# Other order of weight loads and modulation products in a hybrid recurrent/PEER layer, one core

## What is computed

```python
mod = silu(c) @ w_mod + b_mod                       # 6 x 1024 values for each of two condition vectors
sh1, sc1, g1, sh2, sc2, g2 = split(mod, 6)
h = rmsnorm(x, norm1_g) * (1 + sc1) + sh1
xr, yr, xp, ga, gb = split(h @ w_in)                # 1024, 1024, 512, 1024, 1024 columns
xr = dwconv(xr)
hf, hb = rglru(xr, forward), rglru(xr, backward)    # gates by block-diagonal products, then a scan
branch_a = ((hf + hb) * gelu(yr)) @ w_up_rnn
branch_b = pool_mix(xp) @ w_up_pool
m = (sigmoid(ga) * branch_a + sigmoid(gb) * branch_b) @ w_o
x = x + g1 * m
h = rmsnorm(x, norm2_g) * (1 + sc2) + sh2
x = x + g2 * peer(h, wq, keys, u_tab, v_tab)        # product-key top-k, experts
y = rmsnorm(x, final_g)
```

## Time and profile before

| what | us |
|---|---|
| median of three runs | 2393.9 (2392.54 to 2401.06) |
| the profiled execution | 2405.23 |
| its span, first to last instruction | 2403.4 |
| TensorE busy in the span | 2281.8 |
| VectorE busy | 1691.7 |
| ScalarE busy | 817.3 |
| GpSimd busy | 980.9 |

### The profile page before, as it was taken

The page is one execution under the profiler, slowest core; times in us unless marked ns, Lnnn a source line. Parts: engine busy times, 40 slices in busy tenths (PEclk is TensorE's granted clock), DMA queues, the critical chain, the costliest instruction groups (busy, mean ns, idle before and its releaser), DMA issues.

```text
span 2403.4 us, 36139 instructions
## 1 busy us (share of the span) xinstructions
PE 2281.8 (95%) x11708; PEld 1947.9 (81%) x11708; DVE 1691.7 (70%) x3334; ACT 817.3 (34%) x1034; POOL 980.9 (41%) x578
## 2 busy tenths in 40 slices
PE   6799997999999999998999999998999999999995
PEld 2789987999999888786888888886888888888883
DVE  2549996131499999101888998997777777777775
ACT  1445553111323222222544444442222222222221
POOL 0223322222132444443222222225667666676671
PEclk9899998989799999999999999998999999999997
DMA  6412223333422444444688888877888888888881
GB/s 247 177 49 66 62 62 112 117 112 117 123 62 79 138 143 140 137 142 146 218 300 302 308 311 301 313 245 234 271 268 268 271 270 268 268 273 268 267 252 70
DMA packets 232787, 467.29 MB, mean 194 GB/s; under 512 B 115344, under 2 KB 115728, under 8 KB 231056
## 3 DMA queue, kind: packets, MB, share of 16 engines
q1 hardware_dynamic: 176416, 270.82, 36.6%
q0 software_dynamic: 36864, 134.23, 16.1%
q10 hardware_dynamic: 19440, 61.35, 6.4%
HBM read 402.37 MB, written 63.97 MB: 194 GB/s over the span
## 4 chain that ended last, share of the span: by engine, by line
PE 74%; issue 9%; DVE 6%; DMA 5%; POOL 3%; ACT 2%; DVEq 1%; ACTq 0%; SPq 0%; POOLq 0%
PE P L653 30%; PE P L457 19%; PE P L619 15%; POOL wLo L399 3%; PE P L642 3%; DMA rows<-in_u_tab,Eg 3%; PE P L479 3%; PE P L466 1%; PE P L543 1%; DMA gel_scratch<-gel 1%; DMA raw<-in_wblk 1%; PE P L499 1%; DVE ohA L1323 1%; DVE gq L1118 1%; DVE rows L1304 1%
## 5 line engine op out<-in xcount | busy, mean ns | idle before, releaser
L678 ACT ACTIVATE wHi<-raw 128x1024 fp32r<-128x1024 f32 x330 | 346.2, 1049 | 1354.2 <-PE P L653 509.6
L399 POOL TENSOR_TENSOR wLo<-raw,wHi 128x1024 fp32r<-128x1024 f32 x192 | 466.5, 2430 | 417.1 <-ACT wHi L678 416.9
L1366 DVE TENSOR_TENSOR wfLo<-wf,wfHi 128x512 fp32r<-128x512 f32 x128 | 313.8, 2452 | 165.4 <-ACT wfHi L678 165.4
L653 PE MATMUL P<-wfHi,wHi 128*128 128x512 f32 x1024 | 409.7, 400 | 10.2 <-DVE wfLo L1366 10.2
L619 PE MATMUL P<-hHi,wHi 128*128 128x512 f32 x1024 | 411.2, 402 | 3.7 <-DVE wLo L1311 3.2
L619 PE MATMUL P<-hHi,wLo 128*128 128x512 f32 x1024 | 406.3, 397 | 0.0
L653 PE MATMUL P<-wfHi,wLo 128*128 128x512 f32 x1024 | 404.4, 395 | 0.0
L619 PE MATMUL P<-hLo,wHi 128*128 128x512 f32 x1024 | 403.7, 394 | 0.0
L653 PE MATMUL P<-wfLo,wHi 128*128 128x512 f32 x1024 | 402.4, 393 | 0.0
L393 POOL TENSOR_TENSOR wLo<-raw,wHi 128x1024 fp32r<-128x1024 f32 (+1 forms) x76 | 182.6, 2404 | 502.4 <-ACT wHi L678 502.3
L418 POOL DMA_INDIRECT rows<-in_u_tab,Eg x128 | 134.6, 1052 | 357.4 <-DVE rows L1304 336.0
(11 more groups left out here) (172 smaller groups left out, 3264.2 us busy)
## 6 DMA issues: line engine op xcount, KB each, us to landing
raw<-in_ublk SPq DMA_DIRECT2D x128, 512.0 KB, 3.7
raw<-in_v_tab SPq DMA_DIRECT2D x128, 512.0 KB, 3.8
raw<-in_wblk SPq DMA_DIRECT2D x116, 512.0 KB, 3.7
gel_scratch<-gel ACTq DMA_DIRECT2D x128, 256.0 KB, 2.0
gsr<-gel_scratch SPq DMA_DIRECT2D x128, 256.0 KB, 6.2
gate_scratch<-stage ACTq DMA_DIRECT2D x6, 4096.0 KB, 17.0
gsr<-gate_scratch SPq DMA_DIRECT2D x128, 192.0 KB, 5.2
x<-in_xT SPq DMA_DIRECT2D x1, 2560.0 KB, 12.3
```

What stands on the lines that cost most here:

```text
L399: pool.tensor_tensor(wLo[:, j % 2, :], raw[:, j, :], wHi[:, j % 2, :].bitcast(f32), ALU.subtract).then_inc(raw_used[j], 1)
L653: last = nc.tensor.matmul(P[k // 2][:, k % 2, :], w_[:, j % 2, k * 128:(k + 1) * 128], x_[:, j % 2, :], start=(first and a == 0 and b == 0 ...
L678: return nc.scalar.activation(out, in_, f, **kw)
L1366: V.tensor_tensor(wfLo[:, j % 2, :], wf[:, j % 2, :], wfHi[:, j % 2, :].bitcast(f32), ALU.subtract).then_inc(s["wlo_ready"], 1)
```

## The change

- `products()`: `ga` 0 and `ga` 1 stand ahead of the first recurrent gates, right after `xr` 1, and no longer in `beside(0)`. The programs of TensorE and ScalarE follow.
- `after()`: the modulations are spread anew. `ga` 2 to 7 carry two each (16 to 27; before one each, 16 to 21), `upr` 0 to 7 one each (28 to 35; before 22 to 29), `wo` 0 to 7 one each (36 to 43; before two after `wo` 0 and 1, one after the others, 30 to 39). 44 to 47 are left for after `wo` 7 (before 40 to 47).
- `stream()`: the load of a modulation comes two products later in the ring than the product it follows on TensorE (before right behind it).
- `MODB` and `mods` take the new groups (16 to 35, 36 to 39, 40 to 47), and the wait on `mod_read` moves ahead of modulation 40, that is behind product `wo` 4.

```diff
@@ def products():
-    out = [("xp", 0), ("yr", 0), ("xp", 1), ("yr", 1), ("xp", 2), ("gb", 0), ("xp", 3), ("gb", 1), ("xr", 0), ("xr", 1)]
+    out = [("xp", 0), ("yr", 0), ("xp", 1), ("yr", 1), ("xp", 2), ("gb", 0), ("xp", 3), ("gb", 1), ("xr", 0), ("xr", 1),
+           ("ga", 0), ("ga", 1)]
@@ def beside(m):
     if m == 0:
-        return [("xr", 2), ("ga", 0), ("ga", 1), ("upp", 0)]
+        return [("xr", 2), ("upp", 0)]
@@ def after(name, m):
     if name == "ga":
-        return [14 + m] if m >= 2 else []
+        return [12 + 2 * m, 13 + 2 * m] if m >= 2 else []
     if name == "upr":
-        return [22 + m]
-    if name == "wo":
-        return [30 + 2 * m, 31 + 2 * m] if m < 2 else [32 + m]
-    return []
+        return [28 + m]
+    return [36 + m] if name == "wo" else []
@@ def stream():
     out = [("mod", m) for m in range(16)]
+    late = []
     for name, m in products():
         out.append((name, m))
-        out += [("mod", n) for n in after(name, m)]
+        late.append([("mod", n) for n in after(name, m)])
+        if len(late) > 2:
+            out += late[-3]
         if (name, m) == ("wq", 1):
-            out += [("mod", 40 + n) for n in range(8)]
+            out += [("mod", n) for n in range(44, 48)]
@@ def MODB(m):
-    return 0 if 30 <= m < 40 else 1
+    return 0 if 36 <= m < 40 else 1
@@ TensorE
         product("xr", 1, hHi, hLo)
+        product("ga", 0, hHi, hLo)
+        product("ga", 1, hHi, hLo)
@@ TensorE
             product("wo", m, hHi, hLo, settled=S_MG if m == 0 else None)
+            if m == 4:
+                pe.wait_ge(s["mod_read"], 1)
             modulations("wo", m)
             if m:
                 norm_part(1, m - 1)
         norm_part(1, KC - 1)
-        pe.wait_ge(s["mod_read"], 1)
-        for m in range(40, 48):
+        for m in range(44, 48):
             modulation(m)
@@ ScalarE
         xr_out(0)
         xr_out(1)
+        ga_out(0)
+        ga_out(1)
@@ VectorE
-        mods(16, 14)
+        mods(16, 20)
@@ VectorE
-        mods(30, 10)
+        mods(36, 4)
```

## The result

The changed kernel is slower by 0.44%: the ratio of its runs to those of the kernel before is 1.0044, 95% interval 1.003 to 1.0057 (medians 2409.3 and 2399.0 us, 8 runs each). Once more beside the kernel before, later, it gave 1.0035 (1.002 to 1.005). The forecast was +0.7 us, the result some 10. The time, 2409.3, lies above the range that I gave (up to 2407). Of the 14.7 us between it and the forecast (2394.6), 5.1 are the base: the forecast started from the median of three runs, 2393.9, and eight runs gave 2399.0 for the same kernel. Counted from 2393.9, the ratio gives 2404.4.

A forecast was written before the change was run, and what follows sets the result against it. The prediction took TensorE as the bound, with VectorE nearly a second bound in the recurrence. Its terms, 1.2 + 11.5 + 5.1 + 6.6 - 16.7 - 7, gave +0.7 us: a median of 2394.6 us, range 2379 to 2407.

The forecast's parts named there:

- A: Recurrence: two `ga` products ahead of the first gates make it end about 1.2 us late (-5.5 to +6).
- B: Before `ga` 5: modulation 20's load waits for `ga` 5's buffer, then modulations 20 and 21 run; +11.5 us.
- C: Behind `ga` 5, 6 and 7: one more modulation each, all blocks in time; +5.1 us.
- D: Products behind pairs of modulations: two of three pairs on the path lose TensorE's clock; +6.6 us (0 to 9.9).
- E: `wo` stretch: waiting, half clock and two modulations go; -16.7 us, at worst -15.7.
- F: Behind `wo` 7: only four modulations, so `wq` 1 ends 5 to 9 us earlier; -7 us.
- R1: Rival: pairs cost no clock and the two modulations before `ga` 5 run at 1.69; 2384.8 us, chance 0.16.
- R2: Rival: in the recurrence collisions fall apart and TensorE's lead carries through; 2387.9 us, chance 0.14.
- R3: Rival: the ring's new order makes TensorE wait at C's five margins of 2.1 us; 2408 us, chance 0.06.
- R4: Rival: low parts of the last `wo` 0 slices stay late, half of E lost; 2403 us, chance 0.09.

The follow-up runs named there:

- e9: The changed kernel with three `gy` buffers instead of two; ratio 1.0013 to the kernel before.
- e8: The changed kernel with GpSimd making only half of each low part within the recurrence; ratio 0.9995 to the kernel before.
- e2: The kernel before with only `ga` 0 and `ga` 1 moved ahead of the first recurrent gates; ratio 1.0042 to the kernel before.
- e1: The changed kernel with `ga` 0 and `ga` 1 back in `beside(0)`; ratio 1.0007 to the kernel before.
- e5: The changed kernel with modulations 18 to 21 ahead of `ga` 5 in the ring; ratio 1.0012 to the kernel before.
- e3: The changed kernel with only `ga` 0 ahead of the first gates, `ga` 1 back in `beside(0)`; ratio 1.0014 to the kernel before.
- e4: The changed kernel with the second modulation behind `ga` 5, 6 and 7 moved into the middle of the next product; ratio 1.0015 to the kernel before.
- e6: e1 with e5's ring order and every pair's second modulation (17 to 27, odd) inside the next product; ratio 0.9942 to the kernel before.
- e10: e6 with modulation 21 put back behind modulation 20, in the wait before `ga` 5; ratio 0.9931 to the kernel before.

## Why the prediction was wrong

| term | predicted | measured in the profile |
|---|---|---|
| A, the recurrence | +1.2 (-5.5 to +6) | +8.4 |
| B, modulations 20 and 21 | +11.5 | +10.7 |
| `ga` 5 itself | 0 | +0.8 |
| C, moved modulations | +5.1 | +5.1 |
| D, clock behind pairs | +6.6 | +6.5 |
| E, `wo` | -16.7 | -16.8 |
| F, behind `wo` 7 | -7 | -9.1 |
| sum at the end of `wq` 1 | +0.7 | +5.6 |

The terms are differences of stretches of TensorE: A is the end of `ga` 5's low part, B from 416.0 to 426.75 (407.6 to 407.7 before), C and D from the end of `ga` 5 to `wo` 0, 101.6 us against 90.0 (three modulations at 1.68 are C, the rest is D), E from there to the end of the last norm part, 79.3 against 96.1, F the rest, 32.4 against 41.4.

**The step that failed is A.** Its outline was right: VectorE holds the recurrence, its first direction starts six late (181.97, predicted 181.5), and it meets GpSimd's subtractions. Mis-sized were "its lead over the old schedule is 4 to 5 us", "A round is 29.2 us, so block 5 starts 2.9 late", and that the wait at block 6 "swallows part". First the lead, since the rounds hang on it, and then the three places where the 7.2 us between +1.2 and +8.4 arose:

- *The lead of TensorE: 0.1 us instead of 4 to 5.* At block 1's first gates TensorE was 7.5 us ahead of the kernel before (180.28 against 187.83). It then waited 4.45 us at the second gates, not 3, because the table load for the sigmoids stood behind the wait for the direction and came on top. And behind the wait it ran at half clock, which my 8.7 less 3 leaves out: the gates took 4.66 us instead of 2.33. So in blocks 1 and 2 the subtractions stand where they stood before, and only VectorE has moved. (The 8.7 us of time saved were also 0.6 too many, since the idle time is filled only from 0.6 us on.)
- *The start of block 1: 1.1 us.* It lies at 207.54, 3.1 late, not 1.9. TensorE's wait has no part in this, since VectorE runs through from 181.97 to 207.54. Its first direction started 0.5 late, and its second took 0.7 longer than I had, with `gr` at 1.72 us beside a subtraction instead of 0.50.
- *The rounds: 3.0 us.* I had three meetings with subtractions per round, at 4.7 us in all. In blocks 1 and 2 there are three, at 6.1 and 6.5, since they also hit the scans and the first step of a direction, for 1.9 to 2.2 us each; the rounds took 30.4 and 30.8 us. From block 3 on they hit both `gr` and one `gs`, as predicted, at 5.0 us, and the rounds take 29.3. Without any meeting a round of VectorE sums to 24.3 or 24.4 us in both kernels; the kernel before had 4.0 us of meetings and 0.56 of waiting. Block 5 starts 7.1 late.
- *Block 6: 3.1 us.* Instead of 1.7 us being swallowed, 1.4 came on top. The wait of 3.55 us was for ScalarE, and ScalarE's order there has the gelu of `yr` 7 first, which needs block 5 finished. In the kernel before its buffer was free in time; in the changed one it was not, and what is late on VectorE comes back on ScalarE. Block 6 starts 8.4 late. e9 shows it: with the third buffer block 6 starts 4.4 late, and 4.0 us are gone.

e8 shows that the subtractions' length decides whether A stays: with half of it the same kernel ends the recurrence 1.2 us earlier than the kernel before. e2 and e1 show that without the move of the two products the change as a whole is no loss. The upper end that I gave A, 6 us, was too near. Its reason was another one too: no further meeting came in, the three were dearer. That TensorE's lost lead is what set the first two rounds apart is read from the timelines; no run restores the lead alone.

**What was right.** B: the wait is released by the load 3.7 us behind the low part, and e5 removes it (`ga` 5 starts 9.8 us earlier, 7.0 are left at `wq` 1, the rest went to the clock). C and E came out to 0.1 us. D: the term is right, its parts aren't. All three pairs lost the clock, not two, but two of them for 1.6 us instead of 3.3. In the seven profiles that have them (both of the changed kernel, e1, e3, e5, e8, e9) each of the pairs behind `ga` 5, 6 and 7 lost it, at 1.6 to 3.3 us; e4 shows that it is the pairing and not the number of modulations. That D comes so near to +6.6 is luck: three pairs lost where two were charged, and two of them half as much. F came out at 9.1, just beyond its range of 5 to 9. B lay below its sum because the load took 3.7 us and not 4.9.

**The rivals.** R1 (the clock holds) is refuted. The kernel before could not settle it, since 4.7 us of idle time in `wo` 0 stood ahead of its first pair; the changed kernel does, with 8 us at a granted clock of 1.00 (450 to 458) and no idle time ahead of its second pair. The Trainium skill's page "TensorE: Matmul & The Clock Gate", section "Why this matters for your kernels", ties the fall to idle gaps. The trace disagrees: in e4 and the changed kernel TensorE idles nowhere in that stretch, only the pairs differ, and only with them the clock falls. R2 (TensorE leads) is refuted by e3. R3 (loads too late for C's margins) did not occur: no modulation behind `ga` 5 waited for its block; in e6, where modulation 22 needs the buffer of 21, TensorE waited 0.8 us. R4 did not occur either, `wo` 0 has no gap. None of my rivals named what happened, term A beyond its upper bound (8.4 against 6).

## What to carry to other kernels

When an engine has half a microsecond to spare per round, a schedule that shifts another engine's phase by some microseconds is not a small edit: count how long the collisions with GpSimd could be in the worst phase (here 6.5 us per round against 4.0), and use that as the bound. Filling idle time at a stage's start paid nothing here: with two products VectorE, the second bound, started later (the changed kernel), and with one it could not follow (e3). A move in a ring of buffers has to be read at the place that reuses the buffer: modulation 20 waited for the block of `ga` 5 only because it stood four places behind it.

## What the runs showed of the hardware

- VectorE's reciprocal (4.18 us) was never lengthened by a subtraction on GpSimd running beside it; its operations with two inputs, its scans and `TENSOR_SCALAR` were, by 0.8 to 2.2 us each, until 0.3 to 1.1 us behind the end of the subtraction they met. The Trainium skill, page "VectorE: DVE Perf Modes", section "Two Vector instructions with no wait between them", names a read interface shared with GpSimd for operations with two SBUF inputs and for two-port modes. By it an operation with one input outside these modes is free. The reciprocal has one input and stays at 4.18 us in all 14 profiles, so the trace agrees if it runs in none of these modes, which no run here shows.
- Two modulations in a row (32 records of 2 columns, 3.4 us) brought TensorE's clock from 2.4 to 1.2 GHz for part of the product behind them in every profile that has them, without idle time (granted clock 1.00 in the second pair of the changed kernel, 0.80 on average behind it); one alone never did. Two with half a product between them did not in e4 and e10, but once in e6, where a wait of 0.8 us lay between them as well.
- A table load on ScalarE can stand behind the wait of the activation it serves (1.28 us at 191.27, right after the direction that was waited for), and then adds to the wait.
